# Down projection of a Strassen-like split: the sum T3 of two weight blocks made by VectorE instead of by an adding DMA

## The reference, cut to what matters

```python
# x: (1, 512, 2048); D_FF = 5632
h2 = rmsnorm(x, ffn_pre_g)
up = causal_depthwise_conv(h2 @ w_up, conv_f_w, conv_f_b)
u_gate, u_val = jnp.split(up, 2, axis=-1)
f = (jax.nn.gelu(u_gate, approximate=True) * u_val) @ w_down     # the stage that is changed
x = x + rmsnorm(f, ffn_post_g)
e = (p[i] @ w_ple) * jax.nn.sigmoid(x @ w_ple_gate)
x = x + rmsnorm(e, ple_post_g)
```

## Time and profile before

| | us |
|---|---|
| time, median of three runs | 2560.11 (2560.07 to 2562.14) |
| the profiled execution: its time | 2560.32 |
| the profiled execution: its span, first to last instruction | 2558.5 |
| down stage, first to last matmul of `down` | 1895.5 to 2333.2 |

### The profile page before, as it was taken

One profiled execution on the slowest core, in us unless ns is written; L12 is line 12 of the kernel. 1 busy time (PEld: TensorE's weight loads), 2 busy tenths in 40 slices (PEclk: granted clock), 3 DMA queues, 4 the chain that ended last, 5 costly groups with the idle time before them and its releaser, 6 DMA issues. The chain is left out here.

```text
span 2558.5 us, 36047 instructions
## 1 busy us (share of the span) xinstructions
PE 2508.3 (98%) x14244; PEld 2202.3 (86%) x14244; DVE 1838.3 (72%) x2224; ACT 1021.1 (40%) x1197; POOL 184.6 (7%) x261
## 2 busy tenths in 40 slices
PE   8999999999999999999999999999999999998998
PEld 6888888888888887899999999999987878877886
DVE  7888766653334236889889998889988787888434
ACT  5222322252223224444444444444454453555323
POOL 0000000000000000011111111111111101200000
PEclk9999999999999999999999999999999999999999
DMA  4332333232333423467777777777787877965221
GB/s 162 107 101 96 99 99 99 91 116 95 94 98 111 148 95 135 150 183 218 209 189 208 212 221 208 190 209 211 221 275 238 264 233 193 286 216 213 87 99 66
DMA packets 153218, 418.71 MB, mean 164 GB/s; under 512 B 12912, under 2 KB 46704, under 8 KB 152048
## 3 DMA queue, kind: packets, MB, share of 16 engines
q1 hardware_dynamic: 119744, 293.64, 33.8%
q0 software_dynamic: 30928, 118.50, 19.3%
q10 hardware_dynamic: 2400, 4.53, 0.5%
HBM read 379.66 MB, written 36.96 MB: 163 GB/s over the span
## 5 line engine op out<-in xcount | busy, mean ns | idle before, releaser
L1047 ACT ACTIVATE w_hi<-ring_raw 128x1024 fp32r<-128x1024 f32 x426 | 450.2, 1060 | 605.6 <-PE ps L945 389.9
L1458 DVE TENSOR_TENSOR ring_lo<-ring_raw,w_hi 128x1024 fp32r<-128x1024 f32 x426 | 518.0, 1221 | 190.5 <-ACT w_hi L1047 188.9
L1447 DVE TENSOR_TENSOR w_lo<-w_raw,w_hi 128x1024 fp32r<-128x1024 f32 x194 | 236.7, 1223 | 408.7 <-ACT w_hi L1037 408.3
L739 PE MATMUL ps<-xg_hi,w_hi 128*128 128x512 f32 x1024 | 401.6, 392 | 11.9 <-DVE w_lo L1447 11.5
L1037 ACT ACTIVATE w_hi<-w_raw 128x1024 fp32r<-128x1024 f32 x194 | 204.7, 1059 | 520.6 <-PE ps L741 365.2
L741 PE MATMUL ps<-xg_hi,w_lo 128*128 128x512 f32 x1024 | 399.7, 390 | 0.0
L740 PE MATMUL ps<-xg_lo,w_hi 128*128 128x512 f32 x1024 | 399.6, 390 | 0.0
L943 PE MATMUL ps<-s_hi,w_hi 128*128 128x256 f32 x1280 | 361.4, 282 | 2.8 <-issue 2.7
L945 PE MATMUL ps<-s_hi,ring_lo 128*128 128x256 f32 x1280 | 361.7, 283 | 0.0
L944 PE MATMUL ps<-s_lo,w_hi 128*128 128x256 f32 x1280 | 361.2, 282 | 0.0
L943 PE MATMUL ps<-xg_hi,w_hi 128*128 128x256 f32 x960 | 271.0, 282 | 2.4 <-DVE ring_lo L1458 2.4
(11 more groups left out here) (242 smaller groups left out, 4186.9 us busy)
## 6 DMA issues: line engine op xcount, KB each, us to landing
ring_raw<-in_w_up SPq DMA_DIRECT2D x200, 512.0 KB, 4.8
ring_raw<-in_w_down SPq DMA_DIRECT2D x114, 512.0 KB, 4.9
w_raw<-in_w_in SPq DMA_DIRECT2D x112, 512.0 KB, 3.3
ring_raw<-in_w_up POOLq DMA_DIRECT2D x80, 512.0 KB, 6.2
w_raw<-in_w_o SPq DMA_DIRECT2D x32, 512.0 KB, 3.6
ring_raw<-in_w_ple_gate SPq DMA_DIRECT2D x32, 512.0 KB, 3.6
xd_raw<-gx_dram POOLq DMA_DIRECT2D x14, 1024.0 KB, 10.9
gx_dram<-g_sums POOLq DMA_DIRECT2D x44, 256.0 KB, 8.7
```

The lines of the kernel that those rows point to most:

```text
L739: pe.matmul(o, w_hi[:, s, cols], hi, start=start, stop=False)
L1047: f(w_hi[:, (U_S + n) % SLOTS], raw_of(n), ACT.Copy).then_inc(hi_ready, 1)
L1447: dve.tensor_tensor(w_lo[:, s], w_raw[:, u.slot(RAW)], as_f32(w_hi[:, s]), ALU.subtract).then_inc(lo_ready, 1)
L1458: dve.tensor_tensor(low_of_unit(n), raw_of(n), as_f32(w_hi[:, (U_S + n) % SLOTS]), ALU.subtract).then_inc(lo_ready, 1)
```

## The change

T3 is no longer completed by an adding transfer. `down_sums` waits for three landings instead of two and makes three sums instead of two: T3 in place from the two blocks that lie in T3's and T1's buffers, then T1, then T2. The buffer of T1 already holds A, so nothing more is loaded. The 22 calls of `add_unit` in the stage, one for each quad and half, are gone from POOL's queue, with `add_down` itself, and 22 VectorE instructions are new. ScalarE and TensorE keep their instructions; ScalarE's high part of a T3 now waits for `sum_ready` instead of `ring_added`. In the up stage T3 and T1 are still completed by adding transfers.

```diff
@@ -160,12 +160,12 @@
 def adds(n):
 
-    return 1 if mat_of(n) == T3 or mat_of(n) == T1 and n < N_DOWN else 0
+    return 1 if mat_of(n) in (T1, T3) and n < N_DOWN else 0
 
 
 def is_sum(n):
 
-    return mat_of(n) in (T2, T4) or mat_of(n) == T1 and n >= N_DOWN
+    return mat_of(n) in (T2, T4) or mat_of(n) in (T1, T3) and n >= N_DOWN
@@ -632,12 +632,6 @@
-            def add_down(i):
-
-                if i < len(DOWN) and adds(N_DOWN + i):
-                    p, h, mat, q = DOWN[i]
-                    add_unit(N_DOWN + i, w_down[sum(PASSES[:p]) + q, 0, 2 * h + 1])
@@ -663,12 +657,9 @@
             load_blocks(0, T2)
-            add_down(4)
-            add_down(7)
             for i, (p, h, mat, q) in enumerate(DOWN):
                 pair, quads = 2 * p + h, PASSES[p]
                 at, nxt = i - START(p, h), p + 1
-                add_down(i + 8)
                 pool.wait_ge(units_done, U_D + i + 1)
@@ -1461,14 +1452,16 @@
                 q = DOWN[n - N_DOWN][3]
                 dve.wait_ge(ring_in[SLOT[first]], landed(first))
+                dve.wait_ge(ring_in[SLOT[n]], landed(n))
                 dve.wait_ge(ring_in[SLOT[n + 1]], landed(n + 1))
+                dve.tensor_tensor(raw_of(n), raw_of(n), raw_of(n + 1), ALU.add).then_inc(sum_ready, 1)
                 w11 = ring_raw[SLOT[first]][:]
                 dve.tensor_tensor(raw_of(n + 1), raw_of(n + 1), w11, ALU.add).then_inc(sum_ready, 1)
@@
-                dve.wait_ge(ring_added[SLOT[n]], added(n))
+                dve.wait_ge(sum_ready, sums_made(n))
                 dve.tensor_tensor(raw_of(n + 2), raw_of(n), w11, ALU.add).then_inc(sum_ready, 1)
```

## The result

| | before | after |
|---|---|---|
| time, median of six runs each, us | 2560.06 (2558.06 to 2562.14) | 2569.24 (2568.61 to 2570.41) |
| the profiled execution: time / span, us | 2560.32 / 2558.5 | 2569.26 / 2567.4 |
| down stage, start of the first to start of the last unit, us | 434.86 | 441.77 |
| the rest, start of the last unit to the end of the span, us | 228.13 | 229.77 |

The ratio is 1.0036, with an interval of 1.0026 to 1.0045: the change makes the kernel slower, by 9.2 us. The prediction had the sign and its range (2562.4 to 2569.3) just holds the time, but its 5.7 us is too small. The profiled executions differ by 8.9 us, and they split as the table shows: 6.9 in the down stage, 1.6 behind it, and 0.3 ahead of it, which is a scatter of the earlier stages.

The account below looks back on a forecast made before the run. TensorE was taken as bound, its waits set by VectorE's bunched queue. The terms -0.3 + 2.3 - 0.3 + 2.3 + 1.9 = +5.9, stated as +5.7, gave 2565.8 us against the median (2566.0 against the profiled execution), range 2562.4 to 2569.3.

Parts of the forecast that it names:

- What bounds the kernel: Down stage: TensorE is the busy engine, and VectorE's queue decides its waits at a few places where work is bunched.
- First quad, -0.3: Start of the stage: the wait for the adding transfer goes, one new sum comes in; net gain 0.3 us.
- Second to third part, +2.3: Third part's first T2 unit: two new sums in VectorE's unbroken run up to `take_far` cost 2.3 us.
- Inside the third part, -0.3: VectorE's 2.71 us wait for an adding transfer goes, absorbing the next new sum; TensorE gains an estimated 0.3 us.
- Fourth to fifth part, +2.3: Fifth part's first T2 unit: again two new sums in VectorE's run up to `take_far`, costing 2.3 us.
- Fifth to sixth part, +1.9: Sixth part's first T2 unit: two new sums, 2.3 us less 0.4 to spare, cost 1.9 us.
- First to second and third to fourth, nothing: At these passages TensorE did not wait for VectorE, whose pause for ScalarE hides the new sums: no cost.
- Rival 1, the clock: Half-clock stretches behind new waits at 2069.74 and 2224.40 cost 1.7 us each: 2567.5, or 2569.2 with both; chance 0.18.
- Rival 2, half absorbed: VectorE's run gives way, so three passages cost one sum each, not two: +2.7 us, 2562.8; chance 0.25.
- Rival 3, faster: Without adding transfers activations land earlier, ScalarE's pauses close and low parts run ahead: 2555.0 us; chance 0.04.
- Rival 4, no weight: Each of the 22 new sums might fall where TensorE has spare: 2560.1 us; chance 0.03.
- The rule on transfers: Down stage: 22 x 0.5 MB fewer, so other loads land earlier; no TensorE wait ends with a load, sum unchanged.

Follow-up runs that it names:

- e3: Changed kernel with `take_far` moved ahead of the sums of the new part's second quad, nothing else changed: 2562.24 us, ratio to before 1.0006.
- e9: Kernel before with four filling matmuls in the first W22 unit of the sixth part: 2559.91 us, ratio to before 1.0002.
- e10: Kernel before with eight filling matmuls in the first W22 unit of the sixth part: 2561.27 us, ratio to before 1.0009.
- e2: Changed kernel with VectorE's sum only in the six passage quads, adding transfers kept in the other 16: 2566.64 us, ratio to before 1.0026.
- e1: Changed kernel with VectorE's sum in 16 quads, adding transfers kept in the six at passages into parts three, five and six: 2559.4 us, ratio to before 1.0.
- e7: Changed kernel with T2's sum made twice in 14 quads outside the passages: 2570.1 us, ratio to before 1.0035.
- e5: Changed kernel as it is, run and profiled once more: 2568.74 us, ratio to before 1.0036.
- e8: Changed kernel with T2's sum made twice in the six quads at the passages: 2576.44 us, ratio to before 1.0067.
- e11: Changed kernel with eight small filling matmuls ahead of each of the two TensorE waits behind the stage: 2567.69 us, ratio to before 1.0032.
- e4: e1 with `take_far` moved ahead of the sums of the new part's second quad: 2558.02 us, ratio to before 0.9996.
- e6: Changed kernel with eight filling matmuls added to the third unit of parts three and five: 2565.78 us, ratio to before 1.0023.
- e12: e4 with eight small filling matmuls ahead of each of the two TensorE waits behind the stage: 2557.66 us, ratio to before 0.9992.

## Why the prediction came out as it did

**What bounds the kernel: right.** TensorE's wait moved by what VectorE did ahead of four units and by nothing else. e3 shows it best: the same instructions in another order, and 7 us less.

**First quad, -0.3: right against the profile, not in general.** The profile gives -0.39. The step took the landing of one execution, with ScalarE waiting 5.16 us, for the landing. In e9 and e10 it came 2.2 us earlier, and then the term is +1.8. One execution bounds nothing that a transfer ends.

**Second to third part, +2.3: right.** 1.92 at the fourth unit with -0.39 already there makes +2.31, and 1.18 of it appear at the first W11.

**Inside the third part, -0.3: right against the profile, and luck as to its cause.** What after is late by goes from 3.49 us to 3.15 at the quad in question, and VectorE ran through where it had waited 2.71. But every other profile gains 0.3 on before there, e2, e9 and e10 among them, which have the adding transfer at this place and wait for it. The 0.3 is the late landing of one execution, like the first quad's; the missing transfer is not needed for it.

**Fourth to fifth part, +2.3: measured +1.9.** From the part's first unit (3.19 late) to its fourth (5.07) it is 1.88. The two sums are in VectorE's run in full: `take_far` is 21.39 us behind the last pause (2207.12 to 2228.51), where it was 19.12. But the run itself begins 0.4 earlier relative to TensorE. In before the low part of the last W22 began late, 0.47 us behind its high part's end, in after 0.10:

```profile
2184.53 1.23 DVE L1458 TENSOR_TENSOR ring_lo<-ring_raw,w_hi 128x1024 fp32r<-128x1024 f32 x1 [1.86 <-ACT w_hi L1047]
```

```profile
2187.65 1.23 DVE L1449 TENSOR_TENSOR ring_lo<-ring_raw,w_hi 128x1024 fp32r<-128x1024 f32 x1 [1.49 <-ACT w_hi L1038]
```

High parts ended at 2184.06 and 2187.55. e9 and e10 have the 0.47 as before has, e1 has 0.10 and gains 0.39 at that unit. Why the low part begins later there, no row says; e2 has such a delay of 0.47 one low part earlier (high part's end 2186.48, start 2186.95), where it costs nothing.

**Fifth to sixth part, +1.9: right in size.** From 5.06 to 6.91 it is 1.85 (6.78 at the fourth unit, 6.91 from the next unit on).

**First to second and third to fourth, nothing: right.** No new wait appears in either. e7 doubles sums in these parts as well; 0.4 of its 0.7 us have come up by the third part's first unit and 0.3 inside the fourth part.

**The sum.** These terms make +5.4 in the stage, of which the two of -0.3 to -0.4 hold for the one execution of before only. What is missing to 8.9 is 1.55 behind part three's fourth unit, 1.64 behind the stage, and 0.3 of scatter ahead of it. The step that failed is the one that took the clock as it was: the sum priced waits at their own length. A wait here has a second price, the half-speed stretch that may follow it. TensorE's idle time in the stage went from 9.5 to 16.5 us where about 15 was forecast; the slow stretch near 1915, which cost before nothing, is gone, and the one at 2072 costs 1.55.

**Rival 1, the clock: the mechanism was right, its chance too low, its places half wrong.** It named 2069.74 and 2224.40 and 1.7 us each, and priced the first wait at 3.2, which is 2.07 here, since one sum already comes out at the first W11, as the prediction itself allows in its last paragraph. At the first it came, for 1.55, in all six profiled kernels that wait 2 us or more there (after, e2, e5, e7, e8, e11), and in none of the eight others (before, e1, e3, e4, e6, e9, e10, e12). At the second, a wait of 2.24 to 2.26, it came in none of the five; only the 3.92 of e8 brought it. The other 1.6 came in a place that no part of the prediction looked at. That the rival's "2569.2 with both" is the measured time to 0.04 us is luck: one of its two falls was somewhere else. The argument against it was that each wait stands more alone than the pair near 1915. It fits part five, where nothing but the 2.24 stands in the neighbourhood, and not part three, where the split of the two sums had put waits of 1.29 and 0.34 ahead of the 2.07; e3 and e6 have these two as well and no fall, so it takes the long one too. Whether they are what tells the two places apart was not tried, and e8 speaks against a need for such short waits ahead: its waits of 2.54 and 2.38 at the first W11 of parts three and six stand alone as well, and a fall follows each.

**Rival 2, half absorbed: wrong.** Nothing gave way; VectorE's runs grew by 2.26 and 2.27 us for two sums.

**Rival 3, faster: its mechanism does not exist here.** The pauses for ScalarE are as long as before, 0.58 and 0.15, though the adding transfers are gone. e1 has 16 of them gone and the median is 0.8 us lower, inside the interval.

**Rival 4, no weight:** true of 16 sums of the 22 as far as the times can tell, false of the six that count.

**The rule on transfers** gave nothing, as said: the DMA share fell from 0.80 to 0.66, VectorE's waits for landings in these sums from 17.4 us to none, and TensorE's waits grew.

**Open:** whether the short waits ahead are why the 2.07 at part three is followed by a fall of the clock and the 2.24 at part five is not; what decides behind which of the two later waits it comes, if at all; why the first quad's waits brought one in e6 alone; and how much of the scatter of single runs is the landing.

## What to carry to other kernels

Work moved to an engine that keeps the bottleneck fed is not priced by that engine's share but place by place: follow its queue from its last pause to the instruction the bottleneck waits for, and count what has come in between. Here 16 of 22 instructions cost nothing that could be told and six cost nearly all of the stage's loss; the cheap mend was the order in the queue, not fewer instructions (5.7 of 6.9 us). Add to every new wait of TensorE of about 2 us the chance of a stretch at half the clock behind it, and look at more than one execution before pricing a wait that a transfer ends: both gains that the prediction read from such waits were those of one execution.

## What the hardware showed that was not expected

- A wait of TensorE of 2.07 us, whose end came 11.2 and 7.9 us behind those of shorter ones of 1.29 and 0.34, was followed in five traces of five by a stretch of 3.4 us at a granted clock of 0.50. It cost 1.55, near the 1.7 that half of 3.4 is. With 1.8 us of that wait filled by matmuls whose results nobody needs, the stretch stayed away.
- The same does not hold for every wait: 2.24 to 2.26 us at part five brought none in five traces, and 2.65 and 2.84 us behind the stage brought none in before. And the same wait can do either: 1.96 us at the first quad brought a stretch at 0.50 in one trace of ten.
- The same stretch is free if TensorE waits again soon behind it for an engine that was not slowed: the second wait shrank from 2.83 to 1.29.
- One adding transfer of 512 KB, issued at the same place of the same program, let its waiting engine go after 5.16 us in one execution and after 2.88 and 2.96 in two others.
